# The first layer's shift and scale in four blocks of two tiles, its square sums shared by three engines, and a home of its own for the second value chunk

## The reference, cut to what matters

```python
shift, scale, gate = split(silu(c) @ ada_w + ada_b, 3)          # for the latents
shift_c, scale_c, gate_c = split(silu(c_ctx) @ ada_w + ada_b, 3)  # for the context
h  = rmsnorm(x)   * g * (1 + scale)   + shift
hc = rmsnorm(ctx) * g * (1 + scale_c) + shift_c
k = rope(h @ w_k);  v = h @ w_v;  q = rope(h @ w_q);  g = h @ w_g   # the same of hc
y = (attention(q, k, v) * silu(g)) @ w_o
```

## Time and profile before

| what | value |
|---|---|
| median of 3 runs | 1163.66 us (1162.63 to 1164.78) |
| profiled execution, its span | 1164.7 us |
| PE busy | 1102.9 us, 95% |
| DVE, ACT, POOL busy | 726.2, 652.1, 416.5 us |
| span to the end of the key products | 61.54 us |
| HBM traffic | 89 GB/s over the span |

### The profile page before, as it was taken

The page is one execution under the profiler, slowest core; times in us unless marked ns, Lnnn a source line. Parts: engine busy times, 40 slices in busy tenths (PEclk is TensorE's granted clock), DMA queues, the critical chain, the costliest instruction groups (busy, mean ns, idle before and its releaser), DMA issues.

```text
span 1164.7 us, 20187 instructions
## 1 busy us (share of the span) xinstructions
PE 1102.9 (95%) x7408; PEld 899.2 (77%) x7408; DVE 726.2 (62%) x1584; ACT 652.1 (56%) x1363; POOL 416.5 (36%) x513
## 2 busy tenths in 40 slices
PE   4899999999998899999999999999999999999996
PEld 0587787878886589888688887798878777888785
DVE  5475665766668725463688788745766775427745
ACT  4614455545556525653577777846567753457733
POOL 1643112111220243676400001416653335456781
PEclk9899999999999999999999999999999999999999
DMA  8732343513113631131201101052312404213112
GB/s 353 270 144 64 111 171 104 187 64 145 46 28 122 228 105 37 37 108 38 57 10 37 64 10 36 13 164 72 87 37 87 150 19 127 91 55 117 47 37 73
DMA packets 34253, 109.33 MB, mean 94 GB/s; under 512 B 4516, under 2 KB 7076, under 8 KB 33772
## 3 DMA queue, kind: packets, MB, share of 16 engines
q1 hardware_dynamic: 34156, 108.05, 27.6%
HBM read 101.39 MB, written 2.11 MB: 89 GB/s over the span
## 4 chain that ended last, share of the span: by engine, by line
PE 77%; DVE 10%; ACT 5%; issue 3%; POOL 3%; DMA 2%; SPq 0%; POOLq 0%; DVEq 0%; ACTq 0%
PE PS L675 31%; PE PS L658 15%; PE PS L791 8%; PE PS L779 7%; PE PS L975 6%; PE PS L1043 3%; PE PS L710 2%; DMA AF<-wstream 2%; PE PS L876 1%; PE PS L691 1%; DVE AD L2364 1%; ACT AF L1267 1%; POOL AR L2545 1%; DVE AF L1982 1%; POOL AR L2561 1%
## 5 line engine op out<-in xcount | busy, mean ns | idle before, releaser
L2545 POOL TENSOR_TENSOR AR<-AF,AR 128x256 fp32r<-128x256 f32 x396 | 301.7, 797 | 596.3 <-ACT AR L1144 596.3
L675 PE MATMUL PS<-AR 128*128 128x512 f32 (+1 forms) x2208 | 450.4, 360 | 4.7 <-POOL AR L2545 1.4
L675 PEld LDWEIGHTS PS<-AR 128*128 128x128 f32 x2208 | 364.0, 189 | 71.8 <-issue 9.7
L658 PE MATMUL PS<-AR 128*128 128x256 f32 (+4 forms) x1284 | 245.5, 327 | 6.7 <-ACT AF L1267 1.7
L658 PEld LDWEIGHTS PS<-AR 128*128 128x128 f32 (+1 forms) x1284 | 180.3, 190 | 42.1 <-issue 21.7
L1276 ACT ACTIVATE AF<-PS 128x512 f32<-128x512 f32 (+3 forms) x192 | 124.6, 649 | 101.1 <-PE PS L779 97.0
L1267 ACT ACTIVATE AF<-PS,AF 128x512 f32<-128x512 f32 (+3 forms) x192 | 140.8, 734 | 27.1 <-DVE AF L2341 18.3
L779 PE MATMUL PS<-AF 128*128 128x128 f32 x864 | 127.7, 275 | 8.3 <-DVE AF L1982 5.7
L1144 ACT ACTIVATE AR<-AF 128x1024 fp32r<-128x1024 f32 x99 | 103.4, 1052 | 41.4 <-PE PS L975 27.9
L779 PEld LDWEIGHTS PS<-AF 128*128 128x128 f32 x864 | 100.2, 140 | 32.6 <-issue 15.5
L791 PE MATMUL PS<-AF 128*64 128x128 f32 x1728 | 115.8, 279 | 3.1 <-DVE AF L1989 2.2
(11 more groups left out here) (213 smaller groups left out, 1136.4 us busy)
## 6 DMA issues: line engine op xcount, KB each, us to landing
AF<-wstream SPq DMA_DIRECT2D x171, 512.0 KB, 5.1
AF<-x_in SPq DMA_DIRECT2D x2, 1024.0 KB, 8.9
AD<-rows SPq DMA_DIRECT2D x4, 512.0 KB, 5.8
out<-AF SPq DMA_DIRECT2D x16, 128.0 KB, 1.9
AF<-AF SPq DMA_DIRECT2D x28, 64.0 KB, 2.0
AF<-rpb_band SPq DMA_DIRECT2D x8, 224.0 KB, 4.9
BIAS<-rpb_band SPq DMA_DIRECT2D x8, 224.0 KB, 4.7
AF<-ctx_in SPq DMA_DIRECT2D x1, 1024.0 KB, 5.8
```

The source lines that it names most:

```text
L658: mm = pe.matmul(out, stationary, moving, start=i == 0, stop=i == len(products) - 1)
L675: mm = pe.matmul(out[:, 0:t1 - t0], a, b, start=k == 0 and i == 0, stop=k == nk - 1 and i == 2)
L2545: ins = pool.tensor_tensor(w[:, 1, at:at + 256], raw(c)[:, at:at + 256], w[:, 0, at:at + 256].bitcast(F32), ALU.subtract)
```

## The change

1. The columns of the first layer's modulation matrix are put in another order on the host (MODULATION_TILES): ada0.b now holds shift and scale of tiles 2b and 2b + 1, for b = 0 to 3. Each is copied, turned and finished alone; ada_column has two reduces instead of four, and one small add and one gain of a quarter of the channels, done four times instead of twice.
2. Chunk order: ada0.0, A.k0, A.k1, ada0.1, ada0.2, ada0.3, A.v0, A.v1, ada0.4, A.q0, A.g0, ada0.5. The keys' chunks are now the early ones 4 and 5.
3. TensorE's order: half of rows ada0.0 with the context's sum after the first quarter and the latents' sum after the second, the other half, columns ada0.0, rows and columns ada0.1, keys of tile 0, rows ada0.2, keys 1, columns ada0.2, keys 2, rows ada0.3, keys 3, columns ada0.3, keys 4 to 7, rows ada0.4, then as before without columns ada0.5; after the values come rows ada0.5, A.q0.x, columns ada0.5, and the rotation.
4. ACT squares the latents only. DVE squares the whole context in one instruction of 2048 elements a partition, POOL adds these in three (1024, 512 and 256 elements). DVE adds the latents' squares (512 elements, seven times). The root of the context is made and sharpened before that of the latents.
5. A.v1 lives in R3 (R3_HOME), waits for no other weight, and is split right behind A.v0 during the key products: on ACT after tile 5, on POOL after tile 7.

```diff
-ADA_GROUPS = {0: ((0, 2), (1, 3), (4, 5)), 1: (tuple(range(6)),), 2: ((0, 1, 2), (3, 4, 5))}
+ADA_GROUPS = {0: ((0,), (1,), (2,), (3,), (4, 5)), 1: (tuple(range(6)),), 2: ((0, 1, 2), (3, 4, 5))}
@@ chunk_plan
     ada(0, 0)
-    ada(0, 2)
     split("A.k0", "A.k1")
-    ada(0, 1)
-    ada(0, 3)
-    split("A.v0")
+    for b in range(1, 4):
+        ada(0, b)
+    split("A.v0", "A.v1")
     ada(0, 4)
-    split("A.v1")
+    split("A.q0", "A.g0")
     ada(0, 5)
-    split("A.q0", "A.g0")
@@ homes
-    R3_HOME = ["A.o6", "B.o6", "C.o6"]
+    R3_HOME = ["A.v1", "A.o6", "B.o6", "C.o6"]
+        SQCTX = tiles(LOC_[:, 2048:], KD, C)
@@ tensor
-            ada_rows(0, 0)
+            def first_total(name, sums):
+                acc_close(pe.matmul(acc_open(name)[:, 0:sums.shape[-1]], ones, sums, start=True, stop=True), name)
+
+            ada_rows(0, 0, 0, 2)
+            pe.wait_ge(ctx_added, 3)
+            first_total("A.stat.c", RSTD[:, S:T])
+            ada_rows(0, 0, 2, 4)
             pe.wait_ge(sq0_added, KD - 1)
-            for name, sums in (("A.stat.x", RSTD[:, 0:S]), ("A.stat.c", RSTD[:, S:T])):
-                acc_close(pe.matmul(acc_open(name)[:, 0:sums.shape[-1]], ones, sums, start=True, stop=True), name)
-            ada_rows(0, 2)
-            ada_columns(0, 2)
+            first_total("A.stat.x", RSTD[:, 0:S])
+            ada_rows(0, 0, 4, KD)
+            ada_columns(0, 0)
             ada_rows(0, 1)
+            ada_columns(0, 1)
...
             project_together(keys[2:4], h_ready(0), 0, 1)
+            ada_rows(0, 2)
+            project_together(keys, h_ready(0), 1, 2)
+            ada_columns(0, 2)
+            project_together(keys, h_ready(0), 2, 3)
             ada_rows(0, 3)
-            project_together(keys, h_ready(0), 1, 2)
+            project_together(keys, h_ready(0), 3, 4)
             ada_columns(0, 3)
-            project_together(keys, h_ready(0), 2, 4)
+            project_together(keys, h_ready(0), 4, KD)
             ada_rows(0, 4)
-            project_together(keys, h_ready(0), 4, KD)
-            ada_rows(0, 5)
...
                     rotate("A.k1.rot", "A.k1.x", QRAW)
-                    ada_columns(0, 5)
...
-            for name in ("A.q0.x", "A.q0.rot", "A.qg0.c", "A.g0.x"):
+            for name in ("ada0.5", "A.q0.x", "ada0.5.t", "A.q0.rot", "A.qg0.c", "A.g0.x"):
@@ scalar
-            act.wait_ge(sp_x, 32)
+            act.wait_ge(sp_x, 16)
...
-                act.activation(squares[:, 0:S], XL[:, j, :], ACT.Square)
-                act.activation(squares[:, S:T], XC[:, j, :], ACT.Square).then_inc(sq_done, 1)
-            root([("A.stat.x", S, RSTD[:, 0:S]), ("A.stat.c", C, RSTD[:, S:T])])
+                act.activation(squares[:, 0:S], XL[:, j, :], ACT.Square).then_inc(sq_done, 1)
+            root([("A.stat.c", C, RSTD[:, S:T])])
+            root([("A.stat.x", S, RSTD[:, 0:S])])
             feed(2)
...
-                if k == 4:
-                    feed(3)
+                if k == 5:
+                    feed(4)
...
-                    feed(4 + 2 * int(name[3]))
+                    feed(5 + int(name[3]))
@@ vector
+                if len(group) == 1:
+                    for h in range(2):
+                        ins = dve.tensor_reduce(MOD[:, layer, KD * h + 2 * b:KD * h + 2 * b + 2, :], acc[:, 2 * h:2 * h + 2, b],
+                                                AX, ALU.add)
...
+            dve.wait_ge(ctx_in_ready, 16)
+            dve.tensor_tensor(SQCTX, XC, XC, ALU.mult).then_inc(ctx_squared, 1)
             for j in range(1, KD):
                 dve.wait_ge(sq_done, j + 1)
-                signal(dve.tensor_tensor(RSTD, RSTD, SQ[:, j % 2, :], ALU.add), sq0_added, j)
+                signal(dve.tensor_tensor(RSTD[:, 0:S], RSTD[:, 0:S], SQ[:, j % 2, 0:S], ALU.add), sq0_added, j)
+            dve.wait_ge(sp_x, 16)
+            dve.wait_ge(sp_x2, 16)
+            rstd_in_psum((("A.stat.c", C),), RSTD[:, S:T], XN[:, 0, S:T], D)
             ada_row(0, 0)
-            dve.wait_ge(sp_x, 32)
-            dve.wait_ge(sp_x2, 16)
-            rstd_in_psum((("A.stat.x", S), ("A.stat.c", C)), RSTD, XN[:, 0, :], D)
-            ada_row(0, 2)
-            ada_column(0, 2)
+            rstd_in_psum((("A.stat.x", S),), RSTD[:, 0:S], XN[:, 0, 0:S], D)
             for k in range(KD):
-                if k == 2:
-                    ada_row(0, 1)
-                if k == 4:
-                    ada_row(0, 3)
-                    ada_column(0, 3)
+                if k % 2 == 0:
+                    if k:
+                        ada_row(0, k // 2)
+                    ada_column(0, k // 2)
...
-                if j == 0:
-                    ada_row(0, 5)
-                else:
-                    ada_column(0, 5)
...
+            ada_row(0, 5)
+            ada_column(0, 5)
             rope_q(0)
@@ gpsimd
+            pool.wait_ge(ctx_squared, 1)
+            for i, n in enumerate((4, 2, 1)):
+                if i:
+                    pool.wait_ge(ctx_added, i)
+                total = SQCTX[:, 0:n] if n > 1 else RSTD[:, S:T].unsqueeze(1)
+                pool.tensor_tensor(total, SQCTX[:, 0:n], SQCTX[:, n:2 * n], ALU.add).then_inc(ctx_added, 1)
             feed(2)
             for k in range(KD):
                 h_low(0, k, XN0, HA, 0, T)
-                if k == 4:
+                if k == 5:
                     feed(3)
+            feed(4)
             pool.wait_ge(rope_a_in, 16)
             cosine("A.k0.x", QRAW, COSP)
-            feed(4)
+            feed(5)
@@ host
+MODULATION_TILES = [t for b in range(4) for t in (2 * b, 2 * b + 1, KD + 2 * b, KD + 2 * b + 1)] + list(range(16, 24))
```

More of the change, by code:

```diff
@@ L115, in task_plan @@
         task(f"A.stat.{part}", {"x": 4, "c": 5}[part])
-    for name, bank in (("ada0.0", 0), ("ada0.2", 1), ("ada0.2.t", 2), ("ada0.1", 6), ("ada0.3", 2), ("ada0.3.t", 6)):
-        task(name, bank, *filler_chunks(name))
+    for b in range(4):
+        task(f"ada0.{b}", 2, *filler_chunks(f"ada0.{b}"))
+        task(f"ada0.{b}.t", 6)
     for name, bank, *chunks in (
             ("A.k0.x", 3, "A.k0"), ("A.k0.c", 7, "A.k0"), ("A.k1.x", 0, "A.k1"), ("A.k1.c", 1, "A.k1"),
-            ("ada0.4", 2), ("ada0.5", 6), ("A.k0.rot", 4),
+            ("ada0.4", 2), ("A.k0.rot", 4),
             ("A.v.0", 2, "A.v0", "A.v1"), ("A.v.1", 3, "A.v0", "A.v1"), ("A.v.2", 7, "A.v0", "A.v1"),
-            ("A.k1.rot", 4), ("ada0.5.t", 5),
+            ("A.k1.rot", 4),
             ("A.v.3", 2, "A.v0", "A.v1"), ("A.v.4", 3, "A.v0", "A.v1"), ("A.v.5", 7, "A.v0", "A.v1"),
-            ("A.q0.x", 0, "A.q0"), ("A.q0.rot", 1), ("A.qg0.c", 2, "A.q0", "A.g0"), ("A.g0.x", 3, "A.g0")):
+            ("ada0.5", 6), ("A.q0.x", 0, "A.q0"), ("ada0.5.t", 5), ("A.q0.rot", 1), ("A.qg0.c", 2, "A.q0", "A.g0"), ("A.g0.x", 3, "A.g0")):
         task(name, bank, *chunks)
@@ L699, in rotate, with ada_rows @@
                 acc_close(pe.matmul(out, perm, raw, start=True, stop=True), name)
-            def ada_rows(layer, b):
+            def ada_rows(layer, b, k0=0, k1=KD):
                 name = f"ada{layer}.{b}"
-                out = acc_open(name)
+                out = acc_open(name) if k0 == 0 else bank[tasks[name][0]]
                 pe.wait_ge(silc_done, 1)
-                for k in range(KD):
+                for k in range(k0, k1):
                     c = chunk_at[f"{name}.{k // 2}"]
@@ L713, in ada_rows @@
                         mm.then_inc(ada_used, 1)
-                acc_close(mm, name)
+                if k1 == KD:
+                    acc_close(mm, name)
             def ada_columns(layer, b):
@@ L1132, in feed @@
                         act.wait_ge(acc_ready[b], i)
-                    elif name in UB_HOME or name in R3_HOME:
+                    elif name != "A.v1" and (name in UB_HOME or name in R3_HOME):
                         act.wait_ge(s_ready, pair_scored("A", N_PAIR - 1))
-                    else:
+                    elif name in in_ring:
                         r = in_ring.index(name)
@@ L1794, in ada_column @@
                 acc = wait_acc(name).rearrange("p (i g c v) -> p i c v g", i=4, g=4, v=2)
-                mod, bias, gain = (ap.rearrange("p (a h r) -> p a h r", h=2, r=8) for ap in (
+                mod, bias, gain = (ap.rearrange("p (a h r) -> p a h r", h=4, r=4) for ap in (
                     MOD[:, layer].rearrange("p a v -> p (a v)"), col(f"ab{layer}", 0, 48), col(f"ng{layer}", 0, 16)))
-                gains = GAIN[:, layer].rearrange("p (h r) v -> p h (r v)", h=2)
+                gains = GAIN[:, layer].rearrange("p (h r) v -> p h (r v)", h=4)
                 columns = MOD[:, layer].rearrange("p (c i) v -> p i c v", i=4)
                 group = group_of_rows(layer, b)
-                blocks = slice(group[0], b + 1, group[1] - group[0])
-                for i in range(4):
-                    ins = dve.tensor_reduce(columns[:, i, blocks, :], acc[:, i, blocks], AX, ALU.add)
+                if len(group) == 1:
```

(15 more changed lines are left out.)

6 lines of the change are left out of this document (3 added, 3 removed).

## The result

The changed kernel took 1167.45 us (median of 6, 1166.38 to 1168.55) against 1163.65 for before: ratio 1.0027, 95% interval 1.0017 to 1.0038. Run again beside the experiments it took 1165.55 (11 runs) against 1164.19: ratio 1.0012, interval 1.0003 to 1.0020. So it is slower, by 1.4 to 3.8 us by the medians (1.4 to 3.1 by the ratios), where I forecast 2.4 us faster.

What follows compares the result with a forecast made beforehand. TensorE, busy 95% of the span, was taken to bound the kernel, gaining only where it waits. Keys 4.8 us earlier, less 1.2 given back and 1.2 for low clock, left 2.4: 1162.3 span, 1161.2 us forecast, range 1157.8 to 1164.6.

Steps and rivals of the forecast that it cites:

- My slower rival: Key stage: low clock stays throughout in short bursts; 6 us of such work makes the kernel over 0.2% slower, 1166; chance 0.09.
- on the queues: Behind the keys: A.q0's chunk lands near 61 and holds ACT, A.k1.x's copy queued behind, with 7 us to spare.
- The handover: From the keys' end to the start of A.q0's rotation: 28.0 us before, forecast 29.2.
- The reference: Profiled kernel before, keys' end at 61.54; the forecast put the new end at 56.7, 4.8 us earlier.
- The forecast's last step: From profiled span to median: the span stood 1.0 above the runs' median, so 1162.3 became 1161.2.
- The handover to tile 6: Key stage, columns ada0.3 to tile 6's low half: 6.2 us before, 6.0 with two reduces less, ending at 52.0.
- The low spell at tile 0: TensorE's clock low across tile 0's keys, likelier than not; costs 1.0 to 2.4 us, taken as 1.2.
- The statistics: First stage: DVE and POOL take turns adding squares; latents' sum starts at 19.3, normed tile 0 at 25.6 instead of 29.95.
- What I gave back: Keys' end to A.q0's rotation: rows ada0.4 add 1.84, columns ada0.5 take off 0.63; 1.2 us lost.

Runs made afterwards that it cites:

- the split late: The changed kernel with ACT and POOL splitting A.q0 behind the second key block's copy instead of the first's: 1164.04 us, ratio to before 0.9990.
- The kernel kept awake: Changed kernel, A.q0 split late, part of rows ada0.4 between tiles 5 and 6, plus six unused TensorE products before tile 0's keys: 1161.20 us, ratio to before 0.9972.
- the own home alone: The kernel before with only A.v1 in its own home, split behind tile 7, and A.q0 split where it was: 1163.78 us, ratio 0.9991.
- only POOL late: The changed kernel with only POOL's A.q0 split moved behind the second key block's cosine, ACT's part left early: 1166.52 us, ratio to before 1.0019.

## Why the prediction was wrong, step by step

**Which way it went.** I forecast 1161.2 and faster; it was 1167.45 and slower, outside the range. My slower rival (the low clock through the whole key stage) did not happen either: the clock was at 0.93 in the stretch from 36 us and at 1.00 from 38. The loss had a place that none of my cases named.

**The step that failed: "on the queues".** I costed the move of A.q0's split at nothing, and named what it does to ACT's queue and to its chunk's landing. I did not put POOL's four pieces beside DVE's split of key block 0, although shows exactly that pair of engines taking turns and I had used it for the squares. The handover was to be 29.2 us; it was 31.2 in all four traces of the new order in which ACT rounds A.q0 early, and 29.45 with the split late. The same move alone in the kernel before lengthened it from 28.2 to 30.0. Before, POOL's A.q0 came at 74.54, behind DVE's split (66.03 to 73.10), and DVE's chain had next to no slack: TensorE stood 0.04 us for the copy of rows ada0.5, and its next value tile began at 74.36, when DVE's first value copy was done (74.30). Cost: 2.0 us.

**The reference.** I set my sum against 61.54 and carried the whole difference over to the median. That end held a low spell of 1.5 us (8.10 against 6.56) that the four other traces of that order do not have; the usual end is 59.87. I had read the spell and named its price (1.0, as I took three tiles for 7.08 and not 6.56), but left it in the old kernel as if it came every time. Cost: 1.7 us of the gain that I counted. The forecast's last step (1.0 between span and median) was wrong too: 1.8 us lie outside the span, so a span above the median was the sign of an execution that took longer than usual.

**The handover to tile 6.** From columns ada0.3 to the low half of tile 6 I took 6.0; it took 6.9 (48.17 to 55.05), and 7.1 in the change run again. The gain's two small DVE instructions took 0.57 and 0.67 us, and 0.19 and 0.18 in the trace before, inside its total of 6.2. POOL splits A.v0 at just that moment (chain of the changed kernel):

```profile
48.56 0.57 DVE AF L1822
49.15 0.67 DVE AF L1823
```

POOL's four pieces (L2557) run from 48.36 to 51.19. DVE and POOL take turns here a third time; 0.9 us. I had written that this split lies in a gap. No experiment moved it, so this cause is read from the traces alone.

**The low spell at tile 0.** The mechanism was right: it was there in all six traces of kernels with the new order and without the extra products, 3.93 to 4.21 us against 2.36. I took 1.2 and it cost 1.6 to 1.85, and up to 0.5 more in the rows behind it. The kernel kept awake shows the cause: only TensorE's stillness before it was changed. Such a spell is not the new order's alone: tile 0's keys took 3.74 us at a clock of 0.56 in the trace of the own home alone, and in the kernel before run again the clock was at 0.50 from 26 to 32 us, just before them.

**The statistics.** Right in kind: both engines held up, DVE's adds stretched from 0.69 to 1.68 and 1.64. The total started at 18.08 instead of 19.3: DVE's first add ended at 12.22 and not 12.9, as the context landed earlier (POOL began at 9.32, not 9.8), and the turns after it took 0.6 us less than I had summed. Tile 0 was normed at 25.8 (25.6 forecast), its keys at 31.0 (31.0). That these two agree is luck in part: from the total to the normed tile I took 6.3 us, and it took 7.7, with the three sharpening passes at 2.9 us instead of 2.4 and the block's finish at 1.3 instead of 0.9, both beside POOL's split of A.k0 and A.k1.

**What I gave back.** 1.2 us for the moved rows: right within 0.3, as the handover of 29.45 with the late split shows against 27.99 in the kernel before and 28.23 with the own home alone (1.5 and 1.2).

Together, at the rotation: forecast -3.6 + 1.2 (clock) = -2.4; plus 1.7 (reference), 2.0 (key split), 0.9 (tile 6), 0.6 (more for the clock) makes +2.8. Between usual traces it is 89.49 against 87.86, +1.6; the remaining 1.2 came from tile 0's keys 0.3 earlier and from rows and columns issued in less time than the earlier trace rows gave. Behind the rotation nothing more is lost: from it to the end of the span it is 1075.2 and 1074.7 us in the two traces of before, 1075.3 and 1074.9 in the two of the change (1073.2 to 1076.1 over all twelve). The median moved by +1.4 in the session of the second trace. In the first session it moved by 3.8 (3.1 by the ratio); its trace has one more wait, for the last chunk of ada0.3 (44.39 above), which stands in none of the later traces of that order. Whether it came more often in that session stays open: only one execution of it was profiled.

## What to carry to other kernels

When a step is moved, list what runs beside it at the new place on the engine with which it takes turns, not only what is queued behind it: one weight's split, some 7 us earlier, lengthened the handover by 2 us and undid what the reordered start gained. Before a sum is set against a profiled execution, check how its device time stands to the median, and take out of it what one execution alone had, such as a low clock spell. And where TensorE must wait a few microseconds before its main work, try a handful of cheap products in the wait: here six of them gave 2.3 us, and the whole reordering with its late split about 1 by the ratio (0.9990).

## What the runs showed of the hardware

Casts on DVE with one input in SBUF were held up by POOL's subtractions as much as DVE's subtractions were: 0.56 us alone, in most rows 0.97 to 1.02 beside POOL. Copies from PSUM (0.69) and multiplications with one operand in PSUM kept their time beside POOL in the rows read here.

Even an instruction of 8 elements a partition can pay for nearly a whole turn: L1822 took 0.17 us where POOL stood still and 1.26 where POOL was in a subtraction of 768 elements (29.73 to 30.99 in the changed kernel; POOL's subtraction L2573 ends at 30.97). The Trainium skill (SBUF — State Buffer, Who interferes with whom) says that issue order and not the shape of the operation decides who waits; the traces agree, with these 1.26 us.

In the changed kernel TensorE waited from 25.7 to 28.7, with only a column turn and another wait of 1.7 us behind it; the granted clock went from 1.00 to 0.50 (stretch from 30 us), and the first key products took 3.93 to 4.21 us in every trace of the new order without added products; with products in these waits the clock stayed at 1.00. The wait before tile 6 did not do it each time: of 2.74 us in the changed kernel, with the clock at 1.00 after it, and of 2.75 with only POOL late, with 0.62 and 0.53 after it.
